# Cross output, norm, scores and first choice in one stage; first gathers in the norm stage; no GpSimd drain at routing and group borders

## The reference

```python
hf = rmsnorm(x, norm_ffn_g)                       # 512 x 1024
q = (hc @ w_pq).reshape(128, 8, 2, 128)           # chunks of 128 tokens, 8 heads
sc = einsum('thcd,chnd->thcn', q, sub_keys)       # two sets of 128 keys a head
vals, idx = lax.top_k(sc, 16)                     # 16 of each set
cand = vals[:, :, 0, :, None] + vals[:, :, 1, None, :]
top_s, top_c = lax.top_k(cand.reshape(...), 16)   # 16 of the 256 pairs
experts = ...                                     # 16384 experts, 16 per token and head
g = softmax(top_s)
act = gelu(einsum('td,thkd->thk', hc, peer_u[experts]))
x = x + einsum('thk,thkd->td', g * act, peer_v[experts])
```

## Time and profile before

| what | us |
|---|---|
| median of 3 runs | 3009.46 (3005.42 to 3011.15) |
| the profiled execution's own time | 2989.41 |
| its span, first to last instruction | 2987.6 |
| TensorE busy | 2399.5 (80%) |
| VectorE busy | 1746.2 (58%) |
| GpSimd busy | 985.4 (33%) |
| ScalarE busy | 906.0 (30%) |
| indirect gathers (queue 0) | 536.90 MB, 44.4% of the DMA engines' span |
| plain loads and stores (queue 1) | 265.35 MB, 25.3% |

### The profile page before, as it was taken

One profiled execution on the slowest core, in us unless ns is written; L12 is line 12 of the kernel. 1 busy time (PEld: TensorE's weight loads), 2 busy tenths in 40 slices (PEclk: granted clock), 3 DMA queues, 4 the chain that ended last, 5 costly groups with the idle time before them and its releaser, 6 DMA issues. The chain is left out here.

```text
span 2987.6 us, 30208 instructions
## 1 busy us (share of the span) xinstructions
PE 2399.5 (80%) x9721; PEld 1601.4 (54%) x9721; DVE 1746.2 (58%) x3652; ACT 906.0 (30%) x1730; POOL 985.4 (33%) x691
## 2 busy tenths in 40 slices
PE   6997999869876888898885986798547457649897
PEld 4776878758653443343332664475336335427574
DVE  3444311031118988888974588587759878864251
ACT  3443222233312222222221334143224314323232
POOL 2332555343213344344442234324313432320101
PEclk9998999979988999999897997899768778769998
DMA  4321333223108999999999898899789999965553
GB/s 156 99 67 50 95 99 102 82 80 127 56 23 318 397 417 408 416 411 399 402 413 368 315 383 347 339 372 398 299 331 375 414 406 392 389 254 219 215 190 140
DMA packets 255851, 803.85 MB, mean 269 GB/s; under 512 B 18302, under 2 KB 138518, under 8 KB 190183
## 3 DMA queue, kind: packets, MB, share of 16 engines
q0 software_dynamic: 73728, 536.90, 44.4%
q1 hardware_dynamic: 181991, 265.35, 25.3%
HBM read 793.36 MB, written 14.07 MB: 270 GB/s over the span
## 5 line engine op out<-in xcount | busy, mean ns | idle before, releaser
L1335 POOL DMA_INDIRECT gathered<-in_peer_rows,experts x436 | 534.7, 1226 | 912.8 <-DVE x_res L2456 623.4
L1446 PE MATMUL peer_banks<-gathered,peer_diags 128*128 128x512 f32 x720 | 344.4, 635 | 57.7 <-ACT peer_diags L1506 57.6
L78 PE MATMUL group_banks<-group_x_t,group_ring 128*128 128x128 f32 (+1 forms) x2016 | 340.7, 332 | 15.9 <-ACT group_x_t L2268 8.4
L2442 DVE CUSTOM_DVE_ANT_0 gathered<-gathered,late_nat 128x1024 f32<-128x1024 f32 x256 | 316.2, 1238 | 39.6 <-DMA gathered<-in_peer_rows,experts 27.4
L78 PEld LDWEIGHTS group_banks<-group_x_t,group_ring 128*128 128x128 f32 x2016 | 308.3, 209 | 45.9 <-ACT group_x_t L2268 10.8
L2456 DVE SCALAR_TENSOR_TENSOR x_res<-gathered,group_weights,x_res 128x1024 f32<-128x1024 f32 x256 | 329.6, 1288 | 2.5
L1446 PEld LDWEIGHTS peer_banks<-gathered,peer_diags 128*128 128x128 f32 x720 | 144.6, 204 | 248.8 <-issue 248.8
L2082 PE MATMUL group_banks<-group_ring,group_x_t 128*128 128x512 f32 x512 | 235.1, 615 | 21.9 <-DMA group_ring<-in_weights 21.8
L1609 DVE CUSTOM_DVE_ANT_0 peer_product<-gathered,early_nat 128x1024 f32<-128x1024 f32 x180 | 214.9, 1223 | 40.6 <-DMA gathered<-in_peer_rows,experts 40.5
L1446 PE MATMUL peer_banks<-peer_early_gathered,peer_diags 128*128 128x512 f32 x304 | 150.8, 650 | 43.1 <-ACT peer_diags L1506 43.1
L1499 ACT ACTIVATE peer_acts<-peer_dots 128x2 f32<-128x2 f32 x128 | 26.0, 203 | 517.3 <-DVE peer_dots L1609 517.2
(11 more groups left out here) (324 smaller groups left out, 4244.6 us busy)
## 6 DMA issues: line engine op xcount, KB each, us to landing
group_ring<-in_weights SPq DMA_DIRECT2D x270, 512.0 KB, 7.6
mixer_wq<-in_w_in SPq DMA_DIRECT2D x24, 512.0 KB, 4.1
mixer_wk<-in_w_in SPq DMA_DIRECT2D x24, 512.0 KB, 4.3
peer_w<-in_w_pq SPq DMA_DIRECT2D x8, 1024.0 KB, 20.0
gathered<-in_peer_rows,experts POOLq DMA_INDIRECT x436, 11.1
diff_wv<-in_w_in SPq DMA_DIRECT2D x8, 512.0 KB, 4.1
conv_wb<-in_w_in SPq DMA_DIRECT2D x8, 512.0 KB, 4.1
merge_w<-in_w_conv_out SPq DMA_DIRECT2D x8, 512.0 KB, 3.7
```

The lines of the kernel that those rows point to most:

```text
L78: last = nc.tensor.matmul(out, lhsT, rhs, start=n == 0, stop=n == len(pairs) - 1)
L1335: nc.gpsimd.indirect_dma_start(row_buffer(m, r), None, A["peer_rows"], bass.IndirectOffsetOnAxis(ap=at, axis=0))\
L1446: last = nc.tensor.matmul(ps[:, ACC[unit % 2] + half, :], diags[:, r % DIAGS, :], row_buffer(m, r)[:, D + half * BANK:D + (half + 1) * BAN ...
L2442: nc.vector.tensor_tensor_reduce(out=row, in0=row, in1=m.late_nat[:, t % 2, :], scale=1.0, scalar=0.0, op0=ALU.mult, op1=ALU.add, accum_ou ...
```

## The change

Six things are done. (1) `opening_stage` takes the place of the cross output's `residual_stage`. It forms tiles 0 and 1 of the cross output chunk by chunk, norms them, scores head 0 for these 256 tokens and chooses for tile 0; half of tile 2 is formed before the transposes, half behind them, and tile 3 behind the scores. The scores of tile 1 are kept in the space of `experts`. (2) The norm stage still norms all four tiles. GpSimd issues the first 14 gathers in it, before anything else. (3) The routing stage starts with the choice for tile 1 alone. All of head 0's and head 1's queries and scores come between the rows of head 0, with those of head 2 (`SCORES_AT`, `COPIES_AT`, `CHOOSE_AT`, `GATES_AT`, each with an entry for head 0 and one for the others). The choices (0, 2) and (0, 3) move to pairs 5 and 7. (4) The queries of head 0 are made twice: for 256 tokens in the opening stage and again for 512 here. (5) The norm, routing and group stages are built with `no_gpsimd_drain`. (6) `experts` and `shifted` live for the whole program, `early_gathered` from the norm stage on, and `mem_t` ends with the cross stages. The class `Routing` holds the buffers of the scores and `choose`, whose instructions are those of before.

```diff
-def norm_stage(nc, name, m, src, tiles, gain, nat, dst_t, ahead=()):
+def norm_stage(nc, name, m, src, tiles, gain, nat, dst_t, ahead=(), first_rows=None):
...
-        with nc.Block() as block:
+        with nc.Block(no_gpsimd_drain=first_rows is not None) as block:
...
             @block.gpsimd
             def _(pool):
+                if first_rows:
+                    first_rows()
...
+def opening_stage(nc, A, m, cross_t):
...
+        with nc.Block() as block:
+            @block.sync
+            def _(sp):
+                for n in range(2):
+                    sp.dma_start(w[n, 0][:, 0, :], quarter_source(view, n, 0)[:, 0, :]).then_inc(first_loaded[n], 16)
+                for n in range(2):
+                    sp.dma_start(w[n, 0][:, 1:, :], quarter_source(view, n, 0)[:, 1:, :]).then_inc(loaded[n, 0], 16)
+                for n in range(2):
+                    sp.dma_start(w[n, 1][:, :, :], quarter_source(view, n, 1)).then_inc(loaded[n, 1], 16)
+                sp.dma_start(g[:, :], A["norm_ffn_g"].to_broadcast([P, D])).then_inc(gain_loaded, 16)
+                sp.dma_start(b.keys[:, :, :], b.key_view[0:N_KEYS, :, :]).then_inc(routing_loaded, 16)
+                sp.dma_start(b.w[:, :, :], b.w_view[:, :, 0:b.PH]).then_inc(routing_loaded, 16)
...
+            @block.scalar
...
+                for t in range(2):
+                    squares(t)
+                for t in range(2):
+                    root(t)
+                for t in range(2):
+                    copy_half(t)
+                act.wait_ge(keys_turned, 1)
+                nc.scalar.activation(b.keys_t[:, :, :], ps[:, 1, 0:2 * P].rearrange("p (c n) -> p c n", c=2), ACT.Copy)
+                act.wait_ge(q_done, 1)
+                nc.scalar.activation(b.q_t[:, :, :], ps[:, 0, :].rearrange("p (c q) -> p c q", c=2), ACT.Copy).then_inc(operands_ready, 1)
+                act.wait_ge(b.scored, 1)
+                for t, kept in enumerate((b.scores[:, 0, 0, :, :], m.first_scores[:, :, :])):
+                    nc.scalar.activation(kept, ps[:, 2, 2 * t * N_KEYS:2 * (t + 1) * N_KEYS].rearrange("p (c n) -> p c n", c=2), ACT.Copy)\
+                        .then_inc(b.scores_ready, 1)
...
+            @block.vector
...
+                for step in (add, mean_of, scale, copy_half):
+                    for t in range(2):
+                        step(t)
+                add(2)
+                b.choose(nc, dve, m, 0, 0)
+                add(3)
+
+            @block.tensor
...
+                def half(t, n):
+                    for c in range(KC):
+                        last = add_chunk(t, n, c)
+                    return last
...
+                for c in range(KC):
+                    for n in range(2):
+                        pe.wait_ge(split, 2 * c + n + 1)
+                        for t in range(2):
+                            last = add_chunk(t, n, c)
+                            if c == KC - 1 and n == 1:
+                                last.then_inc(done, 1)
+                half(2, 0)
+                turn(0)
+                turn(1)
+                half(2, 1).then_inc(done, 1)
+                pe.wait_ge(h_ready, 4)
+                pe.wait_ge(routing_loaded, 32)
+                b.turn_keys(nc, ps[:, 1, :], m.ident).then_inc(keys_turned, 1)
+                for c in range(2):
+                    last = accumulate(nc, ps[:, 0, c * NEAR:(c + 1) * NEAR], [(b.w[:, k, c * P:(c + 1) * P], h_t[:, k, :]) for k in range(KC)])
+                last.then_inc(q_done, 1)
+                pe.wait_ge(operands_ready, 1)
+                b.score(nc, ps[:, 2, :], (0, 1))
+                half(3, 0)
+                half(3, 1).then_inc(done, 1)
...
-    CHOOSE_AT = (3, 6, 9, 12)
+    SCORES_AT = [(0, 2, 4, 6), (1, 10, 12, 14), (2, 20, 24, 28)], [(2, 2, 8, 18)]
+    COPIES_AT = [(0, 3, 4), (1, 7, 8), (2, 13, 15)], [(2, 7, 11)]
+    CHOOSE_AT = {5: (0, 2), 7: (0, 3), 9: (1, 0), 11: (1, 1), 13: (1, 2), 15: (1, 3)}, {3: (1, 0), 6: (1, 1), 9: (1, 2), 12: (1, 3)}
+    GATES_AT = {8: (0, 1), 12: (1, 0), 16: (1, 1)}, {7: (1, 0), 13: (1, 1)}
...
-        with nc.Block() as block:
+        with nc.Block(no_gpsimd_drain=True) as block:
...
-                for r in range(ROWS_HERE + SLOTS):
+                for r in range(Rows.EARLY_SLOTS, ROWS_HERE + SLOTS):
                     if r < ROWS_HERE and r % TOPK == 0:
                         t, h, _ = row_source(r)
-                        pool.wait_ge(expert_done, h * T + t + 1)
+                        pool.wait_ge(expert_done, h * T + t + 1 - CHOSEN)
                     if r == ROWS_HERE:
-                        pool.wait_ge(expert_done, HEADS * T)
-                    if r >= Rows.EARLY_SLOTS and r % LOT == 0:
+                        pool.wait_ge(expert_done, HEADS * T - CHOSEN)
+                    if r % LOT == 0:
                         pool.wait_ge(m.row_added, row_freed(r + LOT - 1))
...
-                for h in range(2):
-                    query(h, 0)
-                    query(h, 1)
-                    turn_keys(h)
-                    score(h)
                 for r in range(ROWS_HERE):
                     h, at = divmod(r, NT * TOPK)
-                    if h + 2 < HEADS:
-                        if at == 2:
-                            query(h + 2, 0)
-                        if at == 8:
-                            query(h + 2, 1)
-                            turn_keys(h + 2)
-                        if at == 18:
-                            score(h + 2)
+                    for ahead, first_half, second_half, scores in SCORES_AT[min(h, 1)]:
+                        if h + ahead < HEADS:
+                            if at == first_half:
+                                query(h + ahead, 0)
+                            if at == second_half:
+                                query(h + ahead, 1)
+                                turn_keys(h + ahead)
+                            if at == scores:
+                                score(h + ahead)
                     add_row(r)
...
-                choose(0, 0)
-                choose(0, 1)
+                b.choose(nc, dve, m, 0, 1, kept=m.first_scores)
                 softmax(0, 0)
...
-                    if lot == 0:
-                        choose(0, 2)
-                    if lot == 1:
-                        choose(0, 3)
-                    if lot == 4:
-                        softmax(0, 1)
-                    if at in CHOOSE_AT and h + 1 < HEADS:
-                        choose(h + 1, CHOOSE_AT.index(at))
-                    if at == CHOOSE_AT[1] + 2 and h + 1 < HEADS:
-                        softmax(h + 1, 0)
-                    if at == CHOOSE_AT[3] + 2 and h + 1 < HEADS:
-                        softmax(h + 1, 1)
+                    if at in CHOOSE_AT[min(h, 1)]:
+                        ahead, t = CHOOSE_AT[min(h, 1)][at]
+                        if h + ahead < HEADS:
+                            b.choose(nc, dve, m, h + ahead, t, (exp_done, 2 * (h + ahead) + t // 2 - 1) if h + ahead else None)
+                    for ahead, n in gates_at(lot - 1):
+                        softmax(ahead, n)
...
 def group_stage(nc, A, m, number, out):
...
-        with nc.Block() as block:
+        with nc.Block(no_gpsimd_drain=True) as block:
...
-            residual_stage(nc, "cross_out", m, cross_t, A["w_co"][0])
+            opening_stage(nc, A, m, cross_t)
...
+                def first_rows():
+                    for r in range(Rows.EARLY_SLOTS):
+                        gather(nc, A, m, r)
+
+                norm_stage(nc, "ffnnorm", m, m.x, T, A["norm_ffn_g"], nat, h_t, first_rows=first_rows)
```

More of the change, by code:

```diff
@@ L1423, in turn_keys @@
                         pe.wait_ge(scores_ready, 2 * h)
-                    for c in range(2):
-                        last = nc.tensor.transpose(ps[:, KEYS, c * P:(c + 1) * P], keys[:, c, :], m.ident[:, :])
-                    last.then_inc(keys_turned, 1)
+                    b.turn_keys(nc, ps[:, KEYS, :], m.ident).then_inc(keys_turned, 1)
                 def score(h):
@@ L1430, in score @@
                     pe.wait_ge(keys_ready, h + 1)
[L1431 to L1437 removed]
+                    for n in range(2):
+                        b.score(nc, ps[:, SCORES[n], :], (2 * n, 2 * n + 1))
                 def add_row(r):
```

291 lines of the change are left out of this document (188 added, 103 removed).

## The result

Median after: 2983.19 us of 4 runs (2977.82 to 2990.1), beside 3009.07 of before (4 runs): ratio 0.9925, 95% interval 0.9911 to 0.9940. Timed again on another chip, ratio 0.9952 (0.9936 to 0.9968), 2987.36 beside 3000.55. So the change saves 14 to 23 us by the two ratios. The forecast was 17.5 us, 2992.

A forecast was written before the change was run, and what follows sets the result against it. The routing stage was taken to run at its gathers' pace, with a second loss at drained borders. First border 11, second 6.5 and routing 0 sum to 17.5 us off the 3009.46 median: 2992, range 2970 to 3012 (own range 2984 to 3000).

The forecast's parts named there:

- Borders, first: Border after the routing stage: without the drain it opens 17.1 us sooner, of which 11 us (5 to 17) are kept.
- The 6 us: First border: extra delay of the gain vector's load, and so of the input scaling, beside queued gathers.
- Borders, second: Next border: opens 6.9 us sooner, once the last two gathers are issued; taken as 6.5 us (4 to 7).
- Rival C: Group stage: the borders' time comes back there, 6 us remain, 3003; chance 0.12.
- Opening: Interleaved opening stage ends at 873.5, norm starts 14.1 us later at 873.8, gathers start 34.5 us earlier.
- The routing stage at 893: Norm stage: GpSimd's 14 gather issues, 18.7 us, are its longest thing, so routing starts at 893 against 873.5.
- First head: Routing stage's start: VectorE idles 20.6 us for tile 2's scores, the head start is spent; stage gain 0.
- Row 42: Routing stage: its dot begins at 1045.6, against 1042.40 before; between 1040 and 1051 as a sign.
- Gather 54: Routing stage: issued at 1062 against 1061.19; it decides, the DMA queue being full from there in both kernels.
- the zero: Routing stage ends where it did: gain 0, bounds 8 us gained or 6 to 10 lost.
- Rival D: First head serial on TensorE, slower query loads: the stage ends 26 us later, 3018; chance 0.10.
- The saturated run: Routing stage from gather 54 on: DMA queue full in both kernels, so the stage ends where it did.

The follow-up runs named there:

- e3: Kernel before with the GpSimd drain left out at the routing stage's border alone; ratio to before 0.9973, 8 us below it.
- e5: Kernel after with the group stage's load of final_g issued ahead of its two 512 KB ring blocks; ratio to before 0.9928.
- e6: Kernel after with final_g loaded first in the group stage and head 0 routed ahead of row 0; 2964.06 us, ratio to before 0.9876.
- e4: Kernel after with head 0's w_pq and keys loaded in the norm stage, its query, keys and scores computed ahead of row 0; ratio to before 0.9887.
- e8: Kernel after with its first 14 gathers moved to the routing stage's start and head 1's w_pq load left out; ratio to before 0.9948.
- e10: Kernel after with the load of head 1's w_pq left out, gathers still early; ratio to before 0.9957.
- e7: Kernel after with its first 14 gathers issued at the start of the routing stage instead of in the norm stage; ratio to before 0.9995.
- e1: Kernel after with the GpSimd drain put back at the routing and group stages' borders; ratio to before 0.9975, 7.5 us below it.

## Why the prediction was right, point by point

**Borders, first.** The opening at 17.1 us sooner was right: the next stage began 1.7 us after the last add began instead of 18.9, 17.2 less. The scaling was to be 6 us later in its stage and was 8.2 (15.3 in, against 7.1); at TensorE the wait for the scaled tiles shrank by 9.0 of my 11. The 6 us was the mis-sized term. From the last add to VectorE's last work at the second border it is 564.2 us with both drains, 556.2 in e3 and 552.1 in the mean without any, so the first border's gain has grown to 8 to 12 by there, and 11 lies inside that. My reading that the scaling is what holds the rest of the border did not hold: e5 gave 7.5 us of scaling back, B got 1.8 (a quarter), and 0.2 in e6 beside e4.

**Borders, second.** 6.5 was forecast, and the border's idle fell by 7.2 in the kernel after, by 8.4 from e3 to the traces without drains. What I did not price is behind it: 3 to 10 us given back in groups 1 and 2. Rival C, borders' time coming back, is thus true in part, in other groups than I put it. The sum of the term, 17.5, stands beside 16 timed (10 to 22) and 11.5 by traces.

**Opening.** Forecast: opening ends 873.5, norm starts 873.8, gathers from 874, 14 in 19 us. Shown: 871.3, 871.82, 874.48, the last of 14 at 891.73. Net of the 1.55 that all of it began sooner, these are within 2.2 us. One step of the sum was added up wrong by 0.5: the terms given for the transposes lead to 846.3, not 845.8; they ended at 844.6, which is 846.2 net.

**The routing stage at 893 was wrong.** I held that GpSimd's 14 issues would be the longest thing in the norm stage. Its peers started at 885.2 while GpSimd went on issuing until 892.7; this border did not wait for GpSimd to finish its instructions either. (The second border opened at 2156.87, just after GpSimd's last issue ended at 2156.74, so this is no rule for all of them.) The first dot came at 898.54 instead of 902.7.

**First head.** VectorE's idle before the third choice: forecast 20.6, shown 21.4, in two waits. Row 42: forecast 1045.6, shown 1039.49, just below the 1040 I gave. Gather 54: 1062, shown 1056.3. The last add within 6 us of 1604: 1600.96. The DMA share from 915 to 1000 was to be under 0.8 and was 0.82. The term's value was 0 and the table says 1.6 (A, two traces against five), which the spread does not tell from 0.

**But the zero was luck in part: a sum of two large terms that I had not seen.** I wrote that the head start is spent in the first head. It is spent only because the new order otherwise costs as much: with the gathers late, the new opening and first head lose 13 us against before (A 809.0 beside 796.3), since head 1's weights, in the kernel before issued at 895.68 and there by 901, ahead of all gathers, are now loaded in the midst of them. TensorE of the kernel before:

```profile
901.02 14.00 PE L78 MATMUL peer_banks<-peer_h_t,peer_w 128*128 128x512 f32 x32 [1.81 <-DMA peer_w<-in_w_pq]
```

The head start takes that back, by filling the slots early so that the queues have room when that load comes. Without the load (e8 beside e10) the head start gives nothing, -3 us. Rival D named this mechanism (weights that land late move the whole run) and gave it to the kernel after; it sits in e7 instead.

**The saturated run.** From row 42's dot to the last add all fourteen traces take 558.6 to 562.2 us. What I said of gather 54, that from there on the stage's length is fixed, holds in both directions, taken from the kernel after's first trace: 15.6 us late (e7) stayed 15.1 late, 14 sooner (e4) became 15.1 sooner.

By the Trainium skill ("DMA: Bandwidth & Descriptors", Queues, rings and completion order) a DMA engine takes turns between its queues by packet. The load of 1 MB in 1 KB rows took 26.5 us from issue to TensorE beside gathers of 8 KB rows (e7), and at most 12.1 beside few (the kernel after, head 1's load as well). That is what such turns would give, and it agrees so far; no run here shows the packets themselves.

## What to carry to other kernels

Ahead of a long run at the pace of one queue, as the 560 us here, only the moment counts at which that run becomes steady; find the row from which all versions take the same time, and judge each edit by when it reaches that row. A load in narrow rows that shared the DMA engines with wide gathers was five times as slow here as alone (26.5 us beside 5.3), so place such a load where the gathers' slots are full, or ahead of them; an engine that uses the load and also frees the slots stops everything while it waits. A drain at a border held every engine for outstanding gathers (17.7 us); where each gather's data is guarded by its own semaphore, as the rows are here (`m.row_loaded`), leave it out and look at once at which load is late next, since a border's time reached the end only in part.

## What the runs showed that I had not expected

- Without the drain the norm stage's border opened while GpSimd still had instructions to issue: peers at 885.2, its last issue ending at 892.7.
- SyncE's eight bias loads took 17.07 us to issue at the first border beside queued gathers, 4.73 in the kernel before, when the gathers had landed.
- The second choice took 13.3 us from its start to the first dot in one trace of the kernel after (898.54 less 885.24), with pauses of 1.53 and 1.98 us that no semaphore explains, and 13.7 in e1 with pauses of 0.62 and 3.35; it took 9.6 in the kernel after's second trace and in e7, with GpSimd issuing beside it in both. The first dot lay at 88 to 93 us from the opening in all versions with the new opening. What makes the pauses stays open.
- Executions of one kernel on one chip spread by up to 25 us (e7: 2984.8 to 3010.0), and one trace of each kernel put this change at 11.5 us instead of 14 to 23.
